# A sixth buffer for the hidden tiles, a new order of the last down groups, and moved tie sets, waits and stores in a hybrid decoder kernel

## What is computed

```python
def trunk_layer(x, params, l, pos, ssd_conv_prev, ssm_prev, cc_conv_prev, ffn_conv_prev, attend):
    u = x @ params['w_in'][l]
    z, xbc, dt_raw, q, k, v, qi, ki, wi, glu = jnp.split(u, points, axis=-1)
    xbc, ssd_conv_new = causal_dwconv(xbc, ssd_conv_prev, ...)
    ...
    dt = jax.nn.softplus(dt_raw.astype(jnp.float32) + params['ssd_dt_bias'][l].astype(jnp.float32))
    a = -jnp.exp(params['ssd_a_log'][l].astype(jnp.float32))
    y_ssd, ssm_new = ssd_scan(xs, dt, a, bm, cm, ssm_prev.astype(jnp.float32))
    ...
    q, k, qi, ki = rope(q), rope(k), rope(qi), rope(ki)
    y_att = attend(q, k, v, qi, ki, wi)          # top 256 keys by the indexer's score, ties by position
    gl = glu[..., :CC_WIDTH] * jax.nn.sigmoid(glu[..., CC_WIDTH:])
    c, cc_conv_new = causal_dwconv(gl, cc_conv_prev, ...)
    ...
    mix = jnp.concatenate([y_ssd, y_att, y_cc], axis=-1) @ params['w_out'][l]
    x = layer_norm(ALPHA * x + mix, params['ln1_g'][l], params['ln1_b'][l])
    up = x @ params['ffn_w_up'][l]
    up, ffn_conv_new = causal_dwconv(up, ffn_conv_prev, params['ffn_conv_w'][l], params['ffn_conv_b'][l])
    f = (jax.nn.silu(up[..., D_FF:]) * up[..., :D_FF]) @ params['ffn_w_down'][l]
    x = layer_norm(ALPHA * x + f, params['ln2_g'][l], params['ln2_b'][l])
```

## Time and profile before

| | us |
|---|---|
| median of 3 runs | 3609.48 |
| lowest, highest | 3604.8, 3613.21 |
| the profiled execution | 3611.02 |
| its span, first to last instruction | 3609.2 |
| PE busy in it | 3281.7 (91%) |
| PEld busy | 2664.2 (74%) |
| DVE busy | 1898.0 (53%) |
| ACT busy | 1217.4 (34%) |
| POOL busy | 662.6 (18%) |
| TensorE's mean granted clock | 0.939 |

### The profile page before, as it was taken

The page is one execution under the profiler, slowest core; times in us unless marked ns, Lnnn a source line. Parts: engine busy times, 40 slices in busy tenths (PEclk is TensorE's granted clock), DMA queues, the critical chain, the costliest instruction groups (busy, mean ns, idle before and its releaser), DMA issues.

```text
span 3609.2 us, 49866 instructions
## 1 busy us (share of the span) xinstructions
PE 3281.7 (91%) x19418; PEld 2664.2 (74%) x19418; DVE 1898.0 (53%) x3006; ACT 1217.4 (34%) x2262; POOL 662.6 (18%) x663
## 2 busy tenths in 40 slices
PE   7899888887999999999889999887788999999996
PEld 4454456545989999999744544665478999999995
DVE  5579774323664434434454996633247544435336
ACT  3256714234241212212133655241434212212213
POOL 0000000011033333423100000001110433334331
PEclk9899999768999999999989999996799999999998
DMA  3110014216011111111111110241340111111111
GB/s 121 45 35 31 30 32 144 90 47 180 13 36 47 36 53 42 45 50 36 52 40 46 31 35 24 82 127 51 106 133 5 40 50 36 53 47 36 56 36 62
DMA packets 167959, 203.59 MB, mean 56 GB/s; under 512 B 61153, under 2 KB 136226, under 8 KB 166818
## 3 DMA queue, kind: packets, MB, share of 16 engines
q1 hardware_dynamic: 163106, 199.26, 18.4%
q10 hardware_dynamic: 4608, 1.05, 0.1%
HBM read 187.17 MB, written 13.08 MB: 55 GB/s over the span
## 4 chain that ended last, share of the span: by engine, by line
PE 68%; DVE 17%; ACT 8%; issue 3%; DMA 1%; SPq 1%; POOL 0%; ACTq 0%; DVEq 0%; POOLq 0%; PEldq 0%
PE PS L777 43%; PE PS L758 5%; DVE MIX L1740 4%; DVE WORK L1740 3%; PE PS L790 2%; ACT WORK L1510 2%; PE PS L859 2%; DVE WORK L1928 2%; ACT X L1380 2%; PE PS L1160 1%; SPq L440 1%; PE PS L1137 1%; PE PS L817 1%; PE PS L952 1%; PE PS L1147 1%
## 5 line engine op out<-in xcount | busy, mean ns | idle before, releaser
L777 PE MATMUL PS<-WORK_parts,WHIGH_parts 128*128 128x352 f32 x4224 | 865.0, 326 | 36.6 <-POOL WORK_parts L745 17.7
L777 PEld LDWEIGHTS PS<-WORK_parts,WHIGH_parts 128*128 128x128 f32 x4224 | 721.1, 191 | 40.8 <-issue 22.5
L777 PE MATMUL PS<-WORK_parts,RING_parts 128*128 128x352 f32 x3168 | 689.5, 326 | 0.0
L758 PE MATMUL PS<-X,RING 128*128 128x512 f32 (+1 forms) x1824 | 602.2, 493 | 22.7 <-ACT MIX L1450 9.6
L777 PEld LDWEIGHTS PS<-WORK_parts,RING_parts 128*128 128x128 f32 x3168 | 546.4, 189 | 0.0
L758 PEld LDWEIGHTS PS<-X,RING 128*128 128x128 f32 x1824 | 303.9, 193 | 321.3 <-issue 319.1
L1740 DVE SCALAR_TENSOR_TENSOR WORK<-WORK,VEC 128x1072 f32<-128x1072 f32 (+1 forms) x236 | 477.3, 2023 | 8.4
L504 POOL TENSOR_TENSOR RING_parts<-RING,WHIGH_parts 128x1024 fp32r<-128x1024 f32 (+2 forms) x184 | 372.3, 2023 | 444.9 <-ACT WHIGH_parts L1329 444.1
L1329 ACT ACTIVATE WORK<-PS 128x32 f32<-128x32 f32 (+11 forms) x412 | 190.8, 513 | 741.2 <-PE PS L777 584.4
L777 PE MATMUL PS<-X_parts,WHIGH_parts 128*128 128x352 f32 x2016 | 436.7, 325 | 0.0
L1738 DVE TENSOR_SCALAR WORK<-WORK,VEC 128x1072 f32<-128x1072 f32 (+1 forms) x90 | 70.6, 785 | 534.0 <-ACT WORK L1329 534.0
(11 more groups left out here) (327 smaller groups left out, 3804.1 us busy)
## 6 DMA issues: line engine op xcount, KB each, us to landing
RING<-w_up SPq DMA_DIRECT2D x88, 512.0 KB, 3.5
RING<-cache_k SPq DMA_DIRECT2D x256, 128.0 KB, 2.1
RING<-cache_v SPq DMA_DIRECT2D x256, 128.0 KB, 2.1
RING<-w_in SPq DMA_DIRECT2D x46, 512.0 KB, 3.6
RING<-w_down SPq DMA_DIRECT2D x80, 256.0 KB, 2.6
RING<-cache_kidx SPq DMA_DIRECT2D x192, 32.0 KB, 1.7
WORK<-w_out SPq DMA_DIRECT2D x12, 512.0 KB, 6.4
MIX<-xT SPq DMA_DIRECT2D x3, 1408.0 KB, 9.7
```

Of the source, the lines that this page charges most:

```text
L758: mm = pe.matmul(job_psum(n, w, first=first), stationary(k), moving(k)[:, first:first + w], start=k == 0, stop=k == k_tiles - 1)
L777: mm = pe.matmul(thirds(n)[:, third, :], a, x[:, third * THIRD:(third + 1) * THIRD], start=k == 0 and part == 0, stop=k == tiles - 1 and p ...
```

## The change

Seven things, in one edit:

- NHID becomes 6. The sixth buffer of each kind (HID, HIDH, HIDL) lies in the columns of CONST that hold the cosines and sines. So these are loaded again in each layer, behind the first three weights, with a semaphore `angles_loaded` for which DVE waits at "dup".
- In JOBS the last two down groups (4 and 5) stand behind all 44 up products.
- The stores of the two convolution states move from key page 4 to the first query tile in SP's order.
- PE's wait for `smp["kq"]` moves behind `open_chunk(0)`.
- EXPA = exp(a_log) moves on ACT from the opening to the end of stage 3.
- DVE spends 9 nominal us of ties ahead of value tile 21, and none behind value tile 22 (6 before).
- CONST gets a second name for the parts in the other number format; nothing is computed by it.

```diff
-NHID = FG + 1
+NHID = FG + 2
...
-    _end = min(2 * FG * (_g + 1) + 2, 2 * FF)
+    _end = 2 * FF if _g >= GROUPS - 2 else 2 * FG * (_g + 1) + 2
...
-        CONST = sb("CONST", [P, NCONST])
+        CONST, CONST_PARTS = sb_twice("CONST", [P, NCONST])
...
-        HIDH = view(NHID, TOK, parts=True)
+        HIDH = view(NHID - 1, TOK, parts=True)
...
-        HID = view(NHID, TOK)
+        HID = view(NHID - 1, TOK)
...
-        HIDL = view(NHID, TOK, parts=True)
+        HIDL = view(NHID - 1, TOK, parts=True)
+        cos, sin = (slice(CONSTS[n][0], CONSTS[n][0] + TOK) for n in ("cos", "sin"))
+        HIDH = [HIDH[:, b, :] for b in range(NHID - 1)] + [CONST_PARTS[:, cos]]
+        HID = [HID[:, b, :] for b in range(NHID - 1)] + [CONST[:, sin]]
+        HIDL = [HIDL[:, b, :] for b in range(NHID - 1)] + [CONST_PARTS[:, sin]]
...
+                    if n == NSLOT - 1:
+                        sp.dma_start(CONST[:, cos.start:sin.stop], const[:, cos.start:sin.stop]).then_inc(angles_loaded, 16)
...
-                    elif name == ("key", NSLOT):
+                    elif name == ("in", T_Q):
                         sp.wait_ge(saved, 8)
                         store(ssd_out[layer, :, :, :], SSDO[:, :, :])
                         store(cc_out[layer, :, :, :], CCO[:, :, :])
+                    elif name == ("key", NSLOT):
                         sp.wait_ge(stage_done, 4 * 3)
...
                 pe.wait_ge(ssd["da"], 1)
-                pe.wait_ge(smp["kq"], 1)
...
                 open_chunk(0)
+                pe.wait_ge(smp["kq"], 1)
...
                 act.wait_ge(vec_loaded, 16)
-                act.activation(EXPA[:, :], VEC[:, V_ALOG:V_ALOG + SSD_HEADS], ACT.Exp)
...
+                act.activation(EXPA[:, :], VEC[:, V_ALOG:V_ALOG + SSD_HEADS], ACT.Exp)
                 stage.end()
...
                     elif name[0] == "dup":
+                        dve.wait_ge(angles_loaded, 16)
...
                 for n in range(N_IDX, N_A):
+                    if JOBS[n] == ("in", T_V):
+                        spend(9, aside)
                     project(n)
...
-                        spend(2 if j < T_GATE else 0 if j <= T_K else 5 if j < T_Q else 8 if j < T_V else 6, aside)
+                        spend(2 if j < T_GATE else 0 if j <= T_K else 5 if j < T_Q else 8 if j < T_V else 6 if j == T_V else 0, aside)
```

More of the change, by code:

```diff
@@ L378, in build @@
         vec_loaded, hist_loaded, stored = sem("vec_loaded"), sem("hist_loaded"), sem("stored")
+        angles_loaded = sem("angles_loaded")
         vector_step, scalar_step, pool_step = sem("vector_step"), sem("scalar_step"), sem("pool_step")
@@ L744, in _ @@
                         pool.wait_ge(hid_high, t + 1)
-                        pool.tensor_tensor(HIDL[:, b, :], HID[:, b, :], HIDH[:, b, :].bitcast(F32), ALU.subtract).then_inc(hid_low, 1)
+                        pool.tensor_tensor(HIDL[b], HID[b], HIDH[b].bitcast(F32), ALU.subtract).then_inc(hid_low, 1)
                 pool.wait_ge(ffn_saved, 2 * FF)
@@ L1315, in _ @@
                         first = name[1] * FG
-                        split_product(m, lambda k: (HIDH[:, (first + k) % NHID, :], HIDL[:, (first + k) % NHID, :]),
+                        split_product(m, lambda k: (HIDH[(first + k) % NHID], HIDL[(first + k) % NHID]),
                                       lambda k: pe.wait_ge(hid_low, first + k + 1))
@@ L1658, in _ @@
                         act.wait_ge(hid_done, t + 1)
-                        copy(HIDH[:, t % NHID, :], HID[:, t % NHID, :]).then_inc(hid_high, 1)
+                        copy(HIDH[t % NHID], HID[t % NHID]).then_inc(hid_high, 1)
             ln_all("ln2", V_LN2G, V_LN2B, VEC)
@@ L2331, in _ @@
                             await_full(dve, JOB[("down", (t - NHID) // FG, KT - 1)])
-                        acc, h = FACC[:, 1, :], HID[:, t % NHID, :]
+                        acc, h = FACC[:, 1, :], HID[t % NHID]
                         dve.scalar_tensor_tensor(out=h[:, 0:SEQ], in0=acc[:, 0:SEQ], scalar=v(V_FFB + i),
```

## The result

| | before | after |
|---|---|---|
| median | 3611.35 | 3558.07 |
| lowest, highest of 4 runs | 3604.8, 3613.68 | 3555.38, 3561.61 |
| the profiled execution | 3611.02 | 3555.62 |
| its span | 3609.2 | 3553.8 |
| TensorE's mean granted clock | 0.939 | 0.942 |

The ratio is 0.9855, with a 95% interval of 0.984 to 0.9871. The forecast was 3558 us, with a range of 3547 to 3573. It was worked out from a median of 3609.48 us before; with one run more that median is 3611.35.

A forecast was written before the change was run, and what follows sets the result against it. TensorE carries 68% of the chain, so gains lie where it idles or runs at its lower clock. Terms (1) to (6) give 48.7 us, the clock 3: 51.7 off 3611.0, 3559.3, median 1.5 lower: 3558 us, range 3547 to 3573.

The forecast's parts named there:

- (1): End of the gated network: last ups ahead of down group 4 cover the wait for tile 21; gain 21.4 us together.
- (6): Opening: moving EXPA out brings the copy of T_KI 1.49 us earlier a layer; gain 3.0 us.
- (2): Opening: the sixth buffer's reload of cosines and sines lands in time; cost 0, at most 1 us a layer.
- Rival D: Opening: the reload of the angles lands too late and makes the kernel slower, 3611 us and more; chance 0.02.
- (3): Boundary from projection to scan: tie sets moved into VectorE's idle time open the barrier 10.84 us earlier; sum 21.7 us.
- (5): Boundary: with the kq wait moved, the scan's first matmul follows the barrier 1.31 us sooner a layer; 2.6 us.
- (4): Boundary: state stores issued earlier cost 0; left in place, their wait would keep 4.1 us of the gain.
- (7): TensorE's clock behind the shortened idle times at boundary and opening: 0 to 11 us together, 3 taken.
- rival A: The clock stays up at all four short idle times, opening and boundary: 59.7 us gained, 3550 us; chance 0.13.
- B: Scan: page loads and the burst pace it, giving back 24.3 us, 3582 us; chance 0.06 including its smaller form.
- smaller form: Boundary: something keeps the barrier at 531.6; 40.5 us in all, 3569 us; chance within B's 0.06.
- C: Gated network's end: the job order gives nothing, since the stall moves elsewhere; 3579 us; chance 0.04.

The follow-up runs named there:

- the repeat: The changed kernel run again with nothing altered, beside two other kernels on one chip: 3553.2 us, ratio 0.9842 to the kernel before.
- jobs: The changed kernel with the old order of the last two down groups, sixth buffer kept: 3580.24 us, ratio 0.9917 to the kernel before.
- jobs5: The kernel before with the new order of the last two down groups but five buffers: 3599.28 us, ratio 0.9968.
- expa: The changed kernel with EXPA back at the start of the opening: 3566.37 us, ratio 0.9882; run again, 3556.36 us, ratio 0.986.
- late norm: The changed kernel with the conformer norm's mean and variance products one query product later, tie sets respread: 3542.66 us, ratio 0.9805; run again, 3532.57 us.
- kq: The changed kernel with TensorE's wait for kq back ahead of the cumulative sums: 3561.88 us, ratio 0.9852 to the kernel before.
- stores: The changed kernel with the two state stores back behind the fourth key page: 3566.7 us, ratio 0.9881 to the kernel before.
- ties: The changed kernel with tie sets spent as before, none ahead of the first value tile: 3586.48 us, ratio 0.9932 to the kernel before.
- angles: The kernel before with only the per-layer reload of cosines and sines and VectorE's wait at dup added: 3613.49 us, ratio 1.0007.

## Why the prediction was right, point by point

**What bounds the kernel.** The three places that the chain and TensorE's timeline named carry 49.3 of the 55.4 us by which the two profiles differ: 2.7 of idle time in the opening (1.33 and 1.32), 24.3 at the boundary and 22.3 at the end of the gated network. The clock behind the boundary gave 3.9 more, and 2.5 came at the start of the layers, where nothing was moved. That the "issue" at the boundary hid VectorE is shown by the run with the old tie order: 12.87 us idle, with the stores out of the way.

**Where luck helped.** The forecast of the profile was 3559.3 us and the measured one is 3555.6; the medians agree to 0.1 us, which is closer than runs of one kernel do, and the repeat had 3553.2. The sum of the parts holds: 48.7 us forecast for (1) to (6) and 49.3 measured. The clock's term was a guess, and the way it came out, below, was not the way that was argued.

**(1) Order of jobs, 21.4.** Measured 22.3 between the traces and 22.2 in the times of jobs. Group 5 in 23.6 us is met. Of the surplus 0.35 us a layer is chance: in the profile of before one product of group 3 took 6.92 and 6.93 us, in nearly all others of this pace 6.57. That part of the stall would stay without the sixth buffer is shown by jobs5, at 4.83 us. The run jobs shows too that the piece behind the stall is slow beyond its first matmuls: 135 of them took 24.0 to 24.6 us, against 22.1 at full level. The prediction had that in its sum, since it took the whole 34.34 us.

**(2) Angles, 0 to 1.** No cost: ratio 1.0007, with an interval that covers 1, and no landmark of the opening moved. Rival D had 43 us of slack between landing and use against it.

**(3) Ties, 21.7 (10.84 and as much again), and (5) kq, 2.6 (1.31).** Together 24.3 forecast, 24.3 measured; apart, by the counter-runs, 10.85 and 1.30 a layer. The copies of tile 21 moved by 0.3 us against the rotation ahead of them, as said, and nobody waited for them.

**(4) Stores, cost 0.** Right, and its counter-case was under-sized: "keep 4.1 us of the gain" is the idle time alone (4.35 and 3.83 in the trace). The clock adds 2.6 us a layer to it.

**(6) EXPA, 3.0.** 2.65: 1.33 and 1.32 a layer, not 1.49. The prediction added the two durations, 1.28 and 0.21. But the copy had started 1.44 us behind the last index load's issue (64.57 to 66.01, EXPA's row overlapping it), and now starts 0.11 behind it (63.48 to 63.59), not at once: 1.33. The chain from the copy to rotdup is as long as before (8.67 and 8.65 us).

**(7) The clock, 3 taken of 0 to 11.** The term was right in size and wrong in its place, so its size was luck. It was put near the low end because half level followed 15 of 20 idle times of 1.9 to 2.7 us, and it was spread over both places. In fact the boundary gave 1.94 and 1.99 us, all of what there was, since half level had ended 4.3 us behind the first matmul before (the bound of 1.9 took 3.8 us of it). And the opening gave nothing: behind 2.42 us TensorE ran at half level up to about 81 us (stretch, us, busy (instructions), granted clock, DMA share, GB/s):

```profile
72.30:81.30 9.00, 9.00 (x19) 0.50 0.33 74
```

Of the 20 idle times most stand in stages where TensorE waits every few microseconds, and they said little about these two places. But the reason given for rival A, 16 us and more of matmuls ahead, does not part them either. Ahead of the boundary's idle time TensorE had worked for 52 us without a wait (from 471.5), and ahead of the opening's for 40 us (from 29.65). The first was followed by full level in 10 of 10 layers, the second, 2.13 to 2.47 us long, by half level in all 16 layers of the profiles that have EXPA moved. What tells them apart is open.

The other 2.5 us of the opening's stretch lie ahead of the parts that were moved, as shown under the result. In layer two of all 13 profiles the step from the first matmul to the next wait goes with the time at which the clock rose: 9.19 us where half level ended after 2.8 us, 10.85 where it lasted 6.2. All six layers of kernels built on before took 10.4 us or more for this step, against 2 of the 20 layers of kernels built on the changed one. Whether that is chance is not shown; it is no part of what was predicted.

**The rivals.** A needed full level at all four places and got two. B: from its next wait on the scan took 1.0 us longer in layer one and 0.2 in layer two; with the faster start the whole stage got shorter by 1.0 and 1.8 us, so the boundary's gain was not given back. Its smaller form, 3569, was met by undoing the stores, 3566.7. C and D did not occur. The low end of the range, rival A less 4 us, should have read 3546 and not 3547.

## What to carry to other kernels

A wait with a vague releaser ("issue", or a DMA) may hide an engine that ends just ahead of it: look at every engine that joins the barrier, and after moving the last one ask which is next, since here the stores would have kept 6.8 us in each layer, idle time and clock together. A reordering and the buffer that it needs have to be costed together; alone they gave 9 to 12 and 0 us, and 22 as a pair. Cutting an idle time can pay twice, once in itself and once in TensorE's clock behind it: at the boundary the last 1.3 us, from 3.32 to 2.02, brought 1.6 us of clock with them, and in the conformer's norm the clock was a quarter of the gain. In the opening the cut from 3.75 to 2.42 us brought none. So count the clock as a term of its own, with both answers. And a chain's shares by engine can change without the kernel, so compare stretches and not shares.

## What the runs showed of the hardware

TensorE's level behind the boundary, by the idle time there, in all profiles; the stretch is the first scan matmul to the scan's next wait, which is 7.44 us at full level.

| idle time, us | kernels | stretch behind it, us | full level |
|---|---|---|---|
| 2.02 | after and its repeat, jobs, expa and its repeat | 7.43 to 7.44 | 10 of 10 layers |
| 2.33 | late norm and its repeat | 7.44, once 9.08 | 3 of 4 |
| 3.32 | kq | 9.02, 9.06 | 0 of 2 |
| 5.85, 6.37 | stores | 10.15, 10.04 | 0 of 2 |
| 12.87 | ties | 10.19, 10.13 | 0 of 2 |
| 14.16, 14.17 | before, angles, jobs5 | 9.38 to 9.58 | 0 of 6 |

The passage is narrow, and at 2.33 us it fell both ways with the same program. The price does not grow with the idle time: it was 2.6 to 2.8 us behind 6 to 13 us, and 1.9 to 2.1 behind 14. In the opening 2.13 to 2.47 us were followed by half level in 16 of 16 layers, so the length of an idle time alone does not decide, nor do unbroken matmuls ahead of it, 40 us there. The second thing not expected is the pace of down group 3, 5.89 or 6.36 us a product at the same granted clock; with it and the clock's chances, runs of one kernel here lie 6 to 17 us apart, which is more than several of the parts that were to be measured.
